# A bidirectional recurrence in rounds: tensor products regrouped and the round's order rewritten, on one core

## The chip, the cores and the metric

The kernel runs on one core of a Trainium2 chip. The metric is the device time of one execution in microseconds (us). The median of three runs of the kernel before is 2963.27 us (2956.47 to 2969.37).

The core has engines that each run their own instruction queue in order: PE (TensorE, matrix products; its weight loads are listed apart as PEld), DVE (VectorE), ACT (ScalarE), POOL (GpSimd) and SP (SyncE, which issues transfers). They wait for each other only through semaphores. A product reads its operands from SBUF and writes to PSUM, which has eight banks of 128 partitions x 512 fp32 numbers; DVE or ACT then bring it back to SBUF.

## The reference, cut to what matters

Two blocks run one after the other on 512 token rows of 1024 numbers. The change touches only the `rwkv_mixer` of the second block: a delta rule scan over 256 context tokens and then 512 tokens, with 8 heads of 64 numbers, once in each direction. A step is

```python
s_kk = jnp.einsum('bhvk,bhk->bhv', s, kk_t)
s = (s * w_t[:, :, None, :]
     - s_kk[..., None] * (kk_t * a_t)[:, :, None, :]
     + v_t[..., None] * k_t[:, :, None, :])
y = jnp.einsum('bhvk,bhk->bhv', s, inp[5]) if emit else None
```

For the context tokens only the state is needed, for the 512 others y as well. Both directions are summed; group norm, a bonus term and a gate follow (`rwkv_out`).

## The kernel before

The scan is done in chunks of L = 64 tokens: NCH = 12 rounds, numbered c = 0 to 11, each with one chunk of either direction. Rounds 0 to 3 are context; from c = 4 a chunk emits y (`emits(c)`). There are 2 directions x 8 heads = 16 problems of 64 x 64, kept as 8 tiles of 64 columns with two problems in each, one on partitions 0 to 63 and one on 64 to 127 (two of the array's 64-row groups). All products are fp32.

What a round computes, by the program's names (lines are those of the kernel before):

- **Pairs** of chunk n = c + 1, from scaled keys kt and bt (POOL, DVE), scaled directions kap and queries rho (POOL): AT = bt x kap, CT = kt x kap, and if it emits R1 = kt x rho, R2 = bt x rho; kT, bT and vt are the keys and values turned, by products with a 64 x 64 identity (L2138 to L2173). DVE masks CT, R1 and R2 into SBUF (`masked`, L2427) and chooses XT out of AT (L2415); ACT copies AT, kT, bT and vt (L2023).
- **Levels** 1 to 5 of the inverse X of a triangular matrix for chunk c, each a chain: product Y of AT with X (`level_Y`), masked product by DVE (`level_y`, L2440), product W (`level_W`), an addition by DVE (`level_x`, L2448), and a 32 x 32 turn by DVE (L2452). Each comes in two halves d = 0, 1 of four tiles.
- **State** of chunk s = c - 1: G = kap x state + CT x vt, U = X x G, Z = kT x vt + bT x U, the new state (DVE: `state_add`, `state_decay`), and if it emits y = rho x state + R1 x vt + R2 x U. ACT copies G and U into SBUF (L2009), since the next product needs them as an operand.
- **Decays** of chunk c + 2: `lora_pe` (L2120), `logits`, `cumulate`, `key_mix` on DVE, tanh and exp on ACT, products on POOL.

All products come from one helper `tiles` (L2087, the matmul on L2094), called with ALONG or ACROSS. ALONG, the problem on partitions 0 to 63 writes PSUM partitions 0 to 63, ACROSS it writes 64 to 127: in a pair of matmuls ALONG uses the two diagonal 64 x 64 quadrants of the array, ACROSS the two others. `beside` (L2105) interleaves an ALONG product (the levels) with an ACROSS product, a tile of each in turn, so that all four quadrants have work; `alone` runs one product. The order of a round is written out by hand for each engine (`rwkv_pe` from L2274, `rwkv_dve` from L2514, `rwkv_act` from L2053). A round of PE begins with `keep_clock(pe, 2, 4)`, four 128 x 128 products whose result nobody reads (L236).

After the loop PE makes half of a projection, turns the normalised y by 64 products ACROSS with the small identity (L2661), and goes on with the projection.

Of the kernel before, what the change touches and what calls it, by code (L numbers as in the profile page):

```python
# [14 lines left out]
P = 128  # L15
# [83 lines left out]
def hybrid_block_kernel(nc, stream, par, x_t, mod_w, c_rows, vbias, gate_w, masks, ctx_t, rpb, router_w, lora, experts, spill, gates_dram, xs_dram, ys_dram, out):  # L99
    ctx = ExitStack()  # L100
    with ctx:
# [1744 lines left out]
        kap, rho = [take(W8, "b") for _ in range(3)], [take(W8, "b") for _ in range(3)]  # L1846
# [3 lines left out]
        CT, R1, R2 = ([take(W8, "a") for _ in range(2)] for _ in range(3))  # L1850
# [28 lines left out]
        M_BANK = dict(vt=6, AT=4, CT=6, kT=4, bT=5, R1=6, R2=4)  # L1879
        LAST_C = NCH - 1  # L1880
        G_BANK = lambda c: 4 if c == LAST_C else 7
        U_BANK = lambda c: 5 if c == LAST_C else 7
        Y_BANK = lambda c: 6 if c == LAST_C else 7
# [18 lines left out]
        pe_m = Marks("rwkv_pe_pairs", lambda c: ("AT", "CT", "kT", "bT") + (("R1", "R2") if emits(c) else ()) + ("vt",))  # L1902
        pe_l = Marks("rwkv_pe_levels", lambda c: [f"{n}{l}{d}" for l in LV for n in "YW" for d in range(2)])
        pe_s = Marks("rwkv_pe_state", lambda c: ("Gs", "ys", "G", "yv", "U", "y") if c == LAST_C else ("Gs", "G", "U", "Z") + (("ys", "y") if emits(c) else ()))
# [4 lines left out]
        dve_p = Marks("rwkv_dve_decay", lambda c: "t0 t1 cs0 ka0 cs1 ka1 kd0 bt0 kd1 bt1 pl0 pl1".split())  # L1909
        dve_m = Marks("rwkv_dve_pairs", lambda c: ("XT", "X", "CT", "R1", "R2") if emits(c) else ("XT", "X", "CT"))  # L1910
# [26 lines left out]
        def rwkv_pool(pool):  # L1937
# [11 lines left out]
            for c in range(NCH):  # L1949
# [21 lines left out]
                for d in range(2):  # L1971
                    pool.wait_ge(dve_p.sem, dve_p.at(c, f"kd{d}"))
                    if c and d == 0:
                        pool.wait_ge(pe_m.sem, pe_m.at(c - 1, "R1" if emits(c - 1) else "kT"))
                    pool.tensor_tensor(half(kt, d), half(tk, d), half(pinv, d), ALU.mult).then_inc(pool_p.sem, 1)
# [13 lines left out]
        def rwkv_act(act):  # L1989
# [17 lines left out]
            def state_copy(c, name, bank, dst):  # L2007
                act.wait_ge(pe_s.sem, pe_s.at(c, name))
                act.activation(dst, psum[:, bank(c), :], ACT.Copy).then_inc(act_s.sem, 1)  # L2009

            def y_copy(c):
                if first_sum(c):
                    act.wait_ge(pe_s.sem, pe_s.at(c, "y"))
                    for d in range(2):
                        act.activation(y_chunk(c, d), half(psum[:, 7, :], d), ACT.Copy).then_inc(act_s.sem, 1)
# [7 lines left out]
            def pair_copy(c, name, dst):  # L2023
                act.wait_ge(pe_m.sem, pe_m.at(c, name))
                act.activation(dst[c % 2], psum[:, M_BANK[name], :], ACT.Copy).then_inc(act_m.sem, 1)
# [19 lines left out]
            pair_copy(0, "AT", AT)  # L2045
            pair_copy(0, "kT", kT)
            pair_copy(0, "bT", bT)
# [5 lines left out]
            for c in range(NCH):  # L2053
                more, next_too = c + 1 < NCH, c + 2 < NCH
                if c:
                    state_copy(c - 1, "G", G_BANK, Gs)
                pair_copy(c, "vt", vt)
                if c:
                    state_copy(c - 1, "U", U_BANK, Us)
                if more:  # L2060
                    unit(c + 1)
                    pair_copy(c + 1, "AT", AT)
                if next_too:
                    sigmoid_in(c + 2, 0)
                    sigmoid_in(c + 2, 1)
                    decays(c + 2, 0)
                if more:
                    pair_copy(c + 1, "kT", kT)
                if c:
                    y_copy(c - 1)  # L2070
                if more:
                    pair_copy(c + 1, "bT", bT)
                if next_too:
                    decays(c + 2, 1)
                if c + 3 < NCH:
                    lora_in_act(act, c + 3)
            rwkv_before_out_act(act)
            state_copy(LAST_C, "G", G_BANK, Gs)
            state_copy(LAST_C, "U", U_BANK, Us)
            rwkv_out_act(act)  # L2080

        def rwkv_pe(pe):
# [4 lines left out]
            ACROSS, ALONG = 1, 0  # L2087

            def tiles(n, bank, *terms, start=None, at=None, wide=L):
                first = n * L if at is None else at  # L2090
                for i, (way, lhs, rhs) in enumerate(terms):
                    for h in range(2):
                        r, o = ROWS[h], ROWS[h ^ way]
                        ins = pe.matmul(psum[o, bank, first:first + wide], lhs(n)[r], rhs(n)[r],  # L2094
# [1478 lines left out]
```

## Time and profile before

| | |
|---|---|
| median of three runs | 2963.27 us |
| profiled execution, its own time | 2955.09 us |
| its span | 2953.5 us |
| loop of the 12 rounds, from the 20 clock products of round 0 (2050.4) to the projection (2354.0) | 303.6 us |
| PE busy in the span | 2781.9 us, 94% |
| mean granted TensorE clock | 0.983 of full speed |

Busy time is the union of an engine's instructions. The view by stretches (rows 2) gives for each stretch its length, then for PE, PEld, DVE, ACT and POOL the busy time with the number of records, then the granted clock, the busy share of the transfer engines and the GB/s. A row of an engine in order of time gives start, duration, engine, line, operation, operands, shape and count, and in brackets how long the engine sat idle before it and what released it ("issue": nothing that the profile shows). A matmul's record begins where it starts to stream and its end is modelled, so the cost of one in a row of many is read from where the next begins. An fp32 matmul has two records of PE and two of PEld in this trace; a whole-array turn in transpose mode has one and one.

### The profile page before, as it was taken

What the parts mean: (1) busy time and instruction counts of PE and PEld (TensorE: products, weight loads), DVE (VectorE), ACT (ScalarE), POOL (GpSimd) and SP (SyncE); (2) the same over time, 40 slices, a digit from 0 to 9 for tenths busy, and PEclk for the clock granted to TensorE, in tenths of its full rate; (3) what the DMA queues carried; (4) which work ended last, traced back from release to release, by engine and by line L of the source; (5) the groups of instructions that cost most, each with busy time, mean ns of one, the idle gap of its engine ahead of it and who ended that gap; (6) DMA issues with size and microseconds to landing.
All of it is one profiled execution on the core that took longest, in us unless ns stands there. A gap on an engine that the chain in (4) does not pass through costs nothing. (4 is left out here: it accounts for less than half of the span.)

```text
span 2953.5 us, 55577 instructions
## 1 busy us (share of the span) xinstructions
PE 2781.9 (94%) x22194; PEld 2295.2 (78%) x22194; DVE 1782.0 (60%) x2735; ACT 1416.3 (48%) x1906; POOL 885.3 (30%) x535
## 2 busy tenths in 40 slices
PE   9999999989999999999999999899878899999997
PEld 7888877777777878888887788677777777888886
DVE  3114655877999953311165620667766655999995
ACT  4444544565663242344455322445433322888883
POOL 3444463130003434344443224342322233000001
PEclk9999999999999999999999999999999999999998
DMA  3334572111222223323274113232000043999995
GB/s 139 97 95 159 176 273 77 61 48 61 83 89 86 94 64 129 96 97 99 93 255 160 51 58 99 72 108 73 4 4 4 23 141 144 398 411 412 412 412 230
DMA packets 110389, 412.46 MB, mean 140 GB/s; under 512 B 12064, under 2 KB 12080, under 8 KB 109312
## 3 DMA queue, kind: packets, MB, share of 16 engines
q1 hardware_dynamic: 88560, 322.24, 30.4%
q0 software_dynamic: 11136, 48.26, 4.4%
q10 hardware_dynamic: 10512, 39.33, 3.7%
q8 instruction: 141, 2.31, 0.3%
q14 instruction: 40, 0.33, 0.0%
HBM read 370.45 MB, written 39.32 MB: 139 GB/s over the span
## 5 line engine op out<-in xcount | busy, mean ns | idle before, releaser
L219 POOL TENSOR_TENSOR ring_r<-ring,whi 128x1024 fp32r<-128x1024 f32 x241 | 592.6, 2469 | 891.0 <-ACT whi L214 881.8
L231 PE MATMUL psum<-xn_r,whi 128*128 128x512 f32 x1176 | 459.2, 390 | 0.0
L214 ACT ACTIVATE whi<-ring 128x1024 fp32r<-128x1024 f32 x247 | 255.8, 1055 | 398.1 <-DMA ring<-stream 394.6
L229 PE MATMUL psum<-xh,ring_r 128*128 128x512 f32 x936 | 385.2, 412 | 16.5 <-DVE ring_r L219 12.3
L2980 DVE TENSOR_TENSOR er_r<-er,eh 128x1024 fp32r<-128x1024 f32 x268 | 310.4, 1220 | 1.6 <-ACT eh L2969 0.7
L2969 ACT ACTIVATE eh<-er 128x1024 fp32r<-128x1024 f32 x268 | 269.2, 1071 | 44.3 <-DMA er<-experts 43.1
L229 PE MATMUL psum<-ffn_xh,ring_r 128*128 128x512 f32 x672 | 261.4, 389 | 0.0
L230 PE MATMUL psum<-ffn_xh,whi 128*128 128x512 f32 x672 | 261.4, 389 | 0.0
L231 PEld LDWEIGHTS psum<-xn_r,whi 128*128 128x128 f32 x1176 | 221.3, 188 | 47.1
L2094 PE MATMUL psum<-mem 64*64 64x64 f32 (+1 forms) x7744 | 203.3, 223 | 55.3 <-issue 27.5
L2094 PEld LDWEIGHTS psum<-mem 64*64 64x64 f32 x7744 | 188.0, 137 | 69.4 <-issue 44.7
L229 PEld LDWEIGHTS psum<-xh,ring_r 128*128 128x128 f32 x936 | 178.0, 190 | 70.1 <-DVE ring_r L219 15.1
L595 DVE TENSOR_TENSOR gu<-gu,psum 128x512 f32<-128x512 f32 x44 | 30.3, 688 | 333.4 <-ACT gu L570 333.4
L230 PE MATMUL psum<-xh,whi 128*128 128x512 f32 x504 | 197.4, 392 | 0.0
L230 PE MATMUL psum<-xh,whi_h 128*128 128x512 f32 x432 | 171.0, 396 | 0.0
L231 PE MATMUL psum<-xn_r,whi_h 128*128 128x512 f32 x432 | 170.9, 396 | 0.0
L498 DVE TENSOR_TENSOR mem<-mem 128x1024 f32<-128x1024 f32 x64 | 121.6, 1933 | 55.8 <-ACT mem L479 55.5
L3040 PE MATMUL psum<-er_r,xbh 128*128 128x512 f32 x368 | 147.0, 400 | 3.6 <-DVE er_r L2980 2.0
L229 PEld LDWEIGHTS psum<-ffn_xh,ring_r 128*128 128x128 f32 x672 | 126.1, 188 | 26.2
L230 PEld LDWEIGHTS psum<-ffn_xh,whi 128*128 128x128 f32 x672 | 126.1, 188 | 26.1
L3042 PE MATMUL psum<-eh,xbl 128*128 128x512 f32 x368 | 144.7, 393 | 0.0
L3041 PE MATMUL psum<-eh,xbh 128*128 128x512 f32 x368 | 144.3, 392 | 0.0
(532 smaller groups left out, 6041.7 us busy)
## 6 DMA issues: line engine op xcount, KB each, us to landing
ring<-stream SPq DMA_DIRECT2D x311, 512.0 KB, 3.5
er<-experts SPq DMA_DIRECT2D x276, 512.0 KB, 8.7
mem<-mod_w ACTq DMA_DIRECT2D x48, 512.0 KB, 4.3
xs_dram<-zero_row POOLq DMA_DIRECT2D x1, 12288.0 KB, 44.0
xs<-xs_dram SPq DMA_DIRECT2D x23, 512.0 KB, 8.6
ys_dram<-y_t ACTq DMA_DIRECT2D x23, 512.0 KB, 6.6
spill<-resid POOLq DMA_DIRECT2D x2, 2048.0 KB, 27.4
resid<-spill POOLq DMA_DIRECT2D x2, 2048.0 KB, 9.5
```

The costliest lines, as they stand in the source:

```text
L214: act.activation(high_of(part, j), w, ACT.Copy).then_inc(w_hi, 1)
L219: pool.tensor_tensor(ring_r[:, s, :, :], ring[:, s, :, :], f(high_of(part, j)), ALU.subtract).then_inc(w_lo, 1)
L229: pe.matmul(bank, lo[:, b, :], x_hi_, start=start, stop=False, skip_group_check=True)
L230: pe.matmul(bank, hi[:, b, :], x_hi_, start=False, stop=False, skip_group_check=True)
L231: return pe.matmul(bank, hi[:, b, :], x_lo_, start=False, stop=stop, skip_group_check=True)
L498: dve.tensor_tensor(mod_t[at % 2], mod_wb[m % 4], mod_c[:, s, :], ALU.mult).then_inc(mod_mul, 1)
L2094: ins = pe.matmul(psum[o, bank, first:first + wide], lhs(n)[r], rhs(n)[r], start=i == 0 if start is None else start, stop=i == len(terms) ...
L2969: act.activation(eh[:, SLOT[kind] + j, :], er[:, SLOT[kind] + j, :], ACT.Copy).then_inc(e_hi, 1)
L2980: dve.tensor_tensor(er_r[:, at, :], er[:, at, :], f(eh[:, at, :]), ALU.subtract).then_inc(e_lo_dve, 1)
L3040: pe.matmul(bank, x_hi_, lo_[:, cols], start=start, stop=False, skip_group_check=True)
L3041: pe.matmul(bank, x_hi_, hi_[:, cols], start=False, stop=False, skip_group_check=True)
L3042: return pe.matmul(bank, x_lo_, hi_[:, cols], start=False, stop=stop, skip_group_check=True)
```

## The change

`tiles` becomes three helpers. `tiles` keeps the ALONG form. `to_tokens` runs pair i = 0 to 7 of problems, where even i writes ALONG and odd i ACROSS, the two problems of a pair into two neighbouring banks; in the operands that have tokens on partitions (CT, R1, R2, AT, vt, Gs, Us) heads of a pair of tiles therefore lie in another order ("slots"). `to_keys` is its counterpart on the way back. kT and bT are turned by four whole-array transposes each (128 x 128, in transpose mode) instead of 16 products with the small identity. Where a chunk emits, CT and R1 are one product of kt with kap and rho side by side (128 columns: `CR`), and AT and R2 one of bt (`AR`). `keep_clock` at the round's start, and `beside` inside the rounds (but for the last), are gone; Z and y are split into a part that needs U and one that doesn't; `lora_pe` runs one round earlier, at a round's end. DVE and ACT follow: masks and copies read two banks by slots, CR is masked by two operations of 128 x 512, R2 and the choice of XT by two of 128 x 256 each. In `rwkv_out_pe` 16 whole-array transposes take the place of the 64 products.

```diff
-            def tiles(n, bank, *terms, start=None, at=None, wide=L):
+            def tiles(n, bank, lhs, rhs, start=True, at=None, wide=L):
...
+            def to_tokens(i, banks, lhs, rhs, start=True, wide=L, every=L):
+                a, odd = i // 2, i % 2
+                for h in range(2):
+                    n = 2 * a + (h ^ odd)
+                    ins = pe.matmul(psum[ROWS[h ^ odd], banks + h, a * every:a * every + wide], lhs(n)[ROWS[h]], rhs(n)[ROWS[h]],
+                                    start=start, stop=True, skip_group_check=True)
+                return ins
...
+            def turned(bank, src):
+                return lambda a: pe.transpose(psum[:, bank, a * P:(a + 1) * P], src[:, a * P:(a + 1) * P], ident[:, :])
...
+            def pair_CR(c):
+                W(pool_p, c, "kt1")
                 if c:
                     W(act_m, c - 1, "vt")
+                if c >= 2:
+                    W(act_s, c - 2, "U")
+                keys = keys_of(c)
+                return lambda n: to_tokens(n, M_BANKS, of(kt), keys, wide=2 * L if emits(c) else L, every=2 * L)
...
             def state_y_old(c):
                 if c < LAST_C:
-                    W(dve_s, c, "z")
+                    W(act_s, c, "G")
...
             for c in range(NCH):
                 n, s = c + 1, c - 1
-                    keep_clock(pe, 2, 4)
-                    level_Ys(c, 1, state_G_old(s), pe_s)
-                    alone(state_G_new(s), ALL, pe_s)
+                level_Ys(c, 1)
+                if last:
+                    alone(state_G_old(s), ALL, pe_s)
+                level_Ws(c, 1)
+                if last:
+                    alone(state_G_new(s), ALL, pe_s)
+                alone(pair_vt(c), ALL, pe_m)
+                level_Ys(c, 2)
+                if y:
+                    alone(state_y_old(s), ALL, pe_s)
+                level_Ws(c, 2)
+                if last:
+                    alone(state_U(s), ALL, pe_s)
+                level_Ys(c, 3)
+                if more:
+                    alone(pair_CR(n), ALL, pe_m)
+                level_Ws(c, 3)
+                if last:
+                    alone(state_Z_values(s), ALL, pe_s)
+                if y:
+                    alone(state_y_values(s), ALL, pe_s)
+                level_Ys(c, 4)
+                if last:
+                    alone(state_Z(s), ALL, pe_s)
+                level_Ws(c, 4)
+                if y:
+                    alone(state_y(s), ALL, pe_s)
+                if more:
+                    alone(pair_AR(n), ALL, pe_m)
+                level_Ys(c, 5)
+                    level_Ws(c, 5)
+                    if c + 3 < NCH:
+                        lora_pe(c + 3)
+                    alone(pair_kT(n), PAIRS, pe_m)
+                    alone(pair_bT(n), PAIRS, pe_m)
...
             def pair_CR(c):                       # on DVE
+                wait(pe_m, c, "CR")
+                if emits(c - 2):
+                    wait(pe_s, c - 2, "yv")
...
+                    dve.tensor_tensor(to, pairs_of(d)[:, :, :, 0:m], over_slots(mask_CR[:, d, 0:m]), ALU.mult).then_inc(dve_m.sem, 1)
```

First place, PE at the start of a round that emits. Before (L236 are the clock products, 64x32 the levels, `shared,mem` the turn of the values, L2133 the decays' `lora_pe`):

```order
L236 MATMUL psum<-ones 128x128 x4
L2094 MATMUL psum<-mem 64x32 x2
L2094 MATMUL psum<-mem 64x64 x2
...
L2094 MATMUL psum<-mem 64x32 x2
L2094 MATMUL psum<-mem 64x64 x18
L2133 MATMUL psum<-mem,shared 128x64 x16
L2094 MATMUL psum<-mem 64x32 x2
L2094 MATMUL psum<-shared,mem 64x64 x2
...
L2094 MATMUL psum<-mem 64x32 x16
L2094 MATMUL psum<-mem 64x64 x16
```

After (L2111 is `tiles`, L2119 `to_tokens`, L2127 `to_keys`):

```order
L2111 MATMUL psum<-mem 64x32 x16
L2119 MATMUL psum<-mem 64x64 x16
L2111 MATMUL psum<-mem 64x32 x16
L2111 MATMUL psum<-mem 64x64 x16
L2119 MATMUL psum<-shared,mem 64x64 x16
L2111 MATMUL psum<-mem 64x32 x16
L2119 MATMUL psum<-mem 64x64 x16
L2111 MATMUL psum<-mem 64x32 x16
L2111 MATMUL psum<-mem 64x64 x16
L2111 MATMUL psum<-mem 64x32 x16
L2119 MATMUL psum<-mem 64x128 x16
L2111 MATMUL psum<-mem 64x32 x16
```

The clock products, the decays' 16 products and the interleaving are gone from here; each product now stands as a block between two halves of a level.

Second place, PE at the end of the same kind of round, after:

```order
L2119 MATMUL psum<-mem 64x128 x16
L2111 MATMUL psum<-mem 64x32 x32
L2177 MATMUL psum<-mem,shared 128x64 x16
L2132 MATMUL psum<-ident,mem 128x128 x8
L2111 MATMUL psum<-mem 64x32 x16
```

The product of 128 columns is AR, then come both parts of level 5, the decays, now for chunk c + 3, and the eight transposes of kT and bT, where before R1 and R2 were interleaved with level 5.

Third place, DVE from level 3 to level 5. Before (L2417 chooses XT, L2392 and L2390 are `cumulate`, L2429 the masks, L2458 and L2464 the state):

```order
L2440 TENSOR_TENSOR mem<-psum,shared 128x128 x2
...
L2417 COPY_PREDICATED mem<-shared,psum 128x2x256
L2392 SCALAR_TENSOR_TENSOR resid<-mem,zero_row 128x256
L2448 TENSOR_TENSOR mem<-mem,psum 128x16x8 x2
...
L2458 TENSOR_TENSOR mem<-mem,psum 128x512
L2429 TENSOR_TENSOR mem<-psum,shared 128x512
...
L2464 TENSOR_TENSOR mem<-mem 128x512
L2390 SCALAR_TENSOR_TENSOR resid<-mem,zero_row 128x256
L2440 TENSOR_TENSOR mem<-psum,shared 128x4x32 x2
...
```

After (L2445 masks CR, L2451 chooses XT, L2463 masks R2, L2493 and L2499 are the state):

```order
L2412 SCALAR_TENSOR_TENSOR resid<-mem,zero_row 128x256
L2483 TENSOR_TENSOR mem<-mem,psum 128x16x8 x2
...
L2445 TENSOR_TENSOR mem<-psum,shared 128x512 x2
L2475 TENSOR_TENSOR mem<-psum,shared 128x128 x2
...
L2493 TENSOR_TENSOR mem<-mem,psum 128x512
L2499 TENSOR_TENSOR mem<-mem 128x512
L2475 TENSOR_TENSOR mem<-psum,shared 128x4x32 x2
...
L2451 COPY_PREDICATED mem<-shared,psum 128x256 x2
L2463 TENSOR_TENSOR mem<-psum,shared 128x256 x2
L2483 TENSOR_TENSOR mem<-mem,psum 128x4x32 x2
L2456 STREAM_TRANSPOSE mem<-mem 128x2x256
```

The state's two operations now stand before level 5's first, the choice of XT has moved from level 3 to level 5, and the masks of CT and R1 are one pair of operations in level 3.

## Rows read from the trace of the kernel before

**Rows 1.** the page: busy time; PE and granted clock in 40 slices (tenths)

```profile
PE 2781.9 (94%) x22194; PEld 2295.2 (78%) x22194; DVE 1782.0 (60%) x2735; ACT 1416.3 (48%) x1906; POOL 885.3 (30%) x535
PEclk9999999999999999999999999999999999999998
```

**Rows 2.** busy time: rounds 0; 1-2; 3; 4; 5-9; 10; 11; tail

```profile
2050.40:2072.20 21.80, 18.21 (x525) 17.43 (x521) 18.60 (x47) 12.96 (x29) 10.88 (x13) 0.92 0.02 5
2072.20:2114.30 42.10, 35.67 (x1362) 33.27 (x1360) 31.82 (x92) 18.38 (x39) 12.54 (x17) 1.00 0.02 4
2114.30:2136.20 21.90, 18.02 (x749) 16.77 (x745) 16.09 (x47) 9.32 (x21) 8.08 (x11) 1.00 0.02 4
2136.20:2160.90 24.70, 18.51 (x747) 17.07 (x745) 17.14 (x49) 9.25 (x20) 7.86 (x11) 1.00 0.01 4
2160.90:2291.90 131.00, 104.39 (x4204) 97.40 (x4201) 85.90 (x241) 48.70 (x102) 38.70 (x51) 0.99 0.02 5
2291.90:2319.30 27.40, 18.95 (x811) 17.58 (x808) 14.95 (x46) 4.10 (x7) 4.50 (x7) 1.00 0.05 13
2319.30:2344.80 25.50, 22.91 (x694) 20.48 (x694) 15.44 (x41) 9.69 (x13) 12.81 (x8) 0.87 0.02 4
2344.80:2354.00 9.20, 9.09 (x147) 5.91 (x136) 4.05 (x7) 5.06 (x9) 2.32 (x2) 1.00 0.01 2
```

**Rows 3.** waits in the loop: us in total, times, longest

```profile
DVE mem L2448 <- PE psum L2094: 67.7, 56, 4.3
PE psum L2094 <- issue: 30.2, 33, 1.8
DVE mem L2440 <- PE psum L2094: 24.5, 43, 1.7
```

**Rows 4.** PE in order of time: start, us, ..., count, idle before it

```profile
2092.16 1.12 PE L2094 MATMUL psum<-mem 64*64 64x32 f32 x32 [0.80 <-DVE mem L2440]
2093.21 1.16 PE L236 MATMUL psum<-ones 128*128 128x128 f32 x8
...
2095.64 1.15 PE L2094 MATMUL psum<-mem 64*64 64x64 f32 x32 [0.18 <-PE psum L2094]
2096.71 2.00 PE L2133 MATMUL psum<-mem,shared 64*128 64x64 f32 x32
...
2203.87 0.39 PE L2094 MATMUL psum<-mem 64*64 64x64 f32 x8 [1.45 <-issue]
...
2219.29 0.25 PE L2094 MATMUL psum<-mem 64*64 64x32 f32 x2
...
2220.33 4.69 PE L2094 MATMUL psum<-mem 64*64 64x32 f32 x202
...
2365.41 3.95 PE L2661 MATMUL psum<-shared,mem 64*64 64x64 f32 x128
...
2630.30 0.60 PE L3034 MATMUL psum<-ident,hid_t 128*128 128x128 f32 x4
2630.74 1.04 PE L3027 MATMUL psum<-ident,xs 128*128 128x128 f32 x8
```

**Rows 5.** DVE in order of time, round 6

```profile
2195.48 0.29 DVE L2448 TENSOR_TENSOR mem<-mem,psum 128x128 f32<-128x128 f32 x1 [2.59 <-PE psum L2094]
...
2196.94 0.48 DVE L2440 TENSOR_TENSOR mem<-psum,shared 128x128 f32<-128x128 f32 x2
...
2205.96 0.68 DVE L2429 TENSOR_TENSOR mem<-psum,shared 128x512 f32<-128x512 f32 x1
```

**Rows 6.** ACT in order of time, a copy of U

```profile
2197.95 0.60 ACT L2009 ACTIVATE mem<-psum 128x512 f32<-128x512 f32 x1 [1.35 <-PE psum L2094]
```

**Rows 7.** transfer queues over the loop: queue, packets, MB

```profile
q8 instruction: 73, 1.20, 1.7%
```

**Rows 8.** transfers of 2204 to 2226 in 40 slices, GB/s

```profile
GB/s 0 0 30 0 0 0 0 0 0 30 0 0 0 0 15 30 0 0 0 0 0 0 30 0 0 0 0 0 30 0 0 0 0 0 0 30 0 0 0 0
q8 instruction: 6, 0.10, 1.8%
```

More of the change, by code:

```diff
@@ L1845, in hybrid_block_kernel @@
         half = lambda v, d: bd(v[:, 4 * L * d:4 * L * (d + 1)])
-        kap, rho = [take(W8, "b") for _ in range(3)], [take(W8, "b") for _ in range(3)]
+        kap_rho = [take(2 * W8, "b") for _ in range(3)]
+        kap, rho = [v[:, 0:W8] for v in kap_rho], [v[:, W8:2 * W8] for v in kap_rho]
         bt, kt = take(W8, "b"), take(W8, "b")
@@ L1849, in hybrid_block_kernel @@
         XX = [take(2 * W8, "a") for _ in range(2)]
-        CT, R1, R2 = ([take(W8, "a") for _ in range(2)] for _ in range(3))
+        CR = [take(2 * W8, "a").rearrange("p (n w t) -> p n w t", n=8, w=2) for _ in range(2)]
+        R2 = [take(W8, "a") for _ in range(2)]
         kT, bT, vt = ([take(W8, "b") for _ in range(2)] for _ in range(3))
@@ L2085, in rwkv_pe @@
             tile_ = lambda v, n: v[:, n * L:(n + 1) * L]
-            ACROSS, ALONG = 1, 0
-            def tiles(n, bank, *terms, start=None, at=None, wide=L):
+            def tiles(n, bank, lhs, rhs, start=True, at=None, wide=L):
                 first = n * L if at is None else at
[L2091 to L2094, printed above, removed]
-                                        start=i == 0 if start is None else start, stop=i == len(terms) - 1, skip_group_check=True)
-                return ins
+                for r in ROWS:
+                    ins = pe.matmul(psum[r, bank, first:first + wide], lhs(n)[r], rhs(n)[r],
+                                    start=start, stop=True, skip_group_check=True)
+                return ins
@@ L2126, in lora_pe @@
                 W(act_w, c, "lw")
-                for m in range(2):
+                for m in parts:
                     for q in range(4):
@@ L2215, in state_U, with state_Z_values @@
                 W(act_s, c, "G")
[L2216 to L2218 removed]
+                if c < LAST_C:
+                    W(act_m, c + 1, "vt")
+                return lambda n: tiles(n, U_BANK, XT_of(c), of(Gs))
+            def state_Z_values(c):
+                W(dve_p, min(c + 3, NCH - 1), "t1")
+                W(act_m, c, "vt")
+                return lambda n: to_keys(n, Z_BANKS, of(kT[c % 2]), of(vt[c % 2]), start=n < 2)
@@ L2230, in state_y_old, with state_y_values @@
-                return lambda n: tiles(n, Y_BANK(c), (ACROSS, of(rho[c % 3]), of(st[c % 2])), start=n == 0)
-            def state_y_new(c):
-                W(dve_m, c, "R2")
+                return lambda n: to_tokens(n, Y_BANKS(c), of(rho[c % 3]), of(st[c % 2]), start=n < 2)
+            def state_y_values(c):
+                W(dve_m, c, "CR1")
                 W(pe_s, c, "ys")
-                return lambda n: tiles(n, 7, (ALONG, of(R1[c % 2]), of(vt[c % 2])), (ALONG, of(R2[c % 2]), of(Us)), start=False)
@@ L2247, in level_Ys @@
-            def level_Ys(c, l, other=None, done=None):
+                return lambda n: slot_product(n, Y_BANKS(c), of(R2[c % 2]), of(Us))
+            def level_Ys(c, l):
                 for d in range(2):
-                    y = level_Y(c, l, d)
-                    if other is None:
-                        alone(y, (LOW, HIGH)[d], pe_l)
-                    else:
-                        beside(y, (LOW, HIGH)[d], pe_l, other, (LOW, HIGH)[d], done if d else None)
+                    alone(level_Y(c, l, d), (LOW, HIGH)[d], pe_l)
@@ L2255, in rwkv_pe, with level_Ws @@
+            def level_Ws(c, l):
+                for d in range(2):
+                    alone(level_W(c, l, d), LOW, pe_l)
             pe.wait_ge(na_a.sem, na_a.end())
```

389 lines of the change are left out of this document (187 added, 202 removed).

## The prediction

> **What bounds the kernel now.** I read the page first. PE is busy 94% of the span, and the granted clock is at or near full speed in all slices [rows 1], so the whole program is close to PE's speed, and an engine's share says nothing more. Then the view by stretches, which cuts the loop at the clock products that open each round [rows 2]. Here PE is less busy than elsewhere: a context round (1 and 2) takes 21.05 us with PE busy 17.8, a full round (5 to 9, those that make pairs, state and y) 26.2 us with PE busy 20.9. DVE is second with 15.9 and 17.2. So neither is full, and the round is a chain that goes to and fro between them. Nothing of the later program can start before the loop ends, so a round that is shorter by 1 us is 1 us of the kernel.
>
> Third, the waits inside the loop [rows 3]. DVE waits for PE 67.7 us before the additions of the levels and 24.5 before their masks. PE itself sits idle 30.2 us in 33 places where no engine released it. One such place is the 1.45 us before 2203.87 [rows 4]. I take these for the supply of PE's instructions, for three reasons. The queue that carries instructions brings 73 packets of 16 KB into the loop [rows 7]. The records of PE and PEld in the eight stretches add up to 9,239 and 9,210 [rows 2], 253 per packet. And in a dense stretch the packets come at a beat: six in 22 us, 3.7 us apart [rows 8]. A full round has 841 + 841 records, 6.6 packets, hence 24.2 us at that beat, of 26.2. A context round has 681 + 680, 5.3 packets, 19.7 of 21.05. By this reading PE is short of instructions for much of the loop: where four quadrants run interleaved it uses 128 records in 1.04 us (2219.29 to 2220.33, [rows 4]), a packet in 2.1 us, far faster than they come.
>
> The Trainium skill says the contrary in "Runtime: NRT & Kernel Launch", section "Instruction fetch mechanics": blocks of 256 instructions are fetched ahead and the fetch is hidden, because dispatch is slower than the fill. The packet size agrees with the trace (253 records per packet), that it is hidden doesn't (30.2 us of idle time with no releaser). By that rule fewer instructions would bring nothing of themselves, and only the array's time below would count.
>
> **The change part by part, for a full round.** Unit prices on PE, from where the next row begins [rows 4]:
>
> - Half levels, 32 columns ALONG, alone: 32 records (16 matmuls) from 2092.16 to 2093.21, 1.05 us. The other places where I looked gave down to 0.95; I take 1.0.
> - 64 columns ALONG, alone: 2095.64 to 2096.71, 1.07.
> - A level beside an ACROSS product: 64 records in 1.04. So the second product is free there, and a level alone costs as much as a level with company.
> - `to_tokens` and `to_keys`, 16 matmuls that alternate the diagonals: not in the trace. The order of quadrants is that of `beside`, 32 matmuls in 1.04, hence 0.53 for 16. Upper bound 1.07, if they don't overlap. I take 0.53, since the quadrants follow each other in the same way.
> - The same with 128 columns (CR, AR): not in the trace. Lower bound 0.53 (as 64 columns), upper 2.1 (twice the price of 64 alone). Columns count: four 128-column clock products take from 2093.21 to about 2094.3, 0.27 each, and there would be four groups of four quadrants; I take 1.07.
> - Decays: 1.9 to 2.0 as before, only moved. Whole-array transpose: four from 2630.30 to 2630.74, 0.11 each, so kT and bT cost 0.87 for the eight.
>
> Sum of PE, before: clock products 1.1; level 1 first half with G old 1.05; G new 1.07; decays 1.95; vt, AT, CT, kT, bT, R1, R2 and old y beside levels, 8 x 1.05 with the split levels counted; U 1.0; Z of two ACROSS terms beside level 3 2.1; level 2 alone 1.0; new y 2.1. That is 19.8, and rows 2 have 20.9, so this way of counting may be 1 us low, for the new round too; that lies in the range. After: ten levels 10.0; G old, vt, old y, both parts of Z 5 x 0.53 = 2.65; G new, U, y from values, y from U 4.3; CR and AR 2.15; decays 1.95; transposes 0.87. Together 21.9. **So the array's work does not fall; it rises by about 1 us.** Instructions do: 360 products of which 8 have half the records, 1,424 against 1,684. That is 5.6 packets, 20.6 us at 3.7 us each, under the 21.9 of the array. The supply stops being the longer of the two.
>
> What remains to wait. DVE has 17.2 + 0.2 (masks in halves) a round, below PE's 21.9, and its idle time costs nothing. CR needs Us copied by ACT, 0.2 + 0.60 [rows 6] behind the tanh pair of the next decays; level 3's first half of 1.0 on PE covers most of it. DVE's mask of CR waits for y from values; behind it stand level 4's masks, for which PE waits some 0.3. I put 0.4 on such dependencies and 0.9 (the mean of the 33 idle places, 30.2 / 33) on one supply gap: a full round takes 21.9 + 1.3 = 23.2. DVE's idle time before additions falls from single waits like 2.59 us [rows 5], since a level's two products are now split by one block, not by decays and two state products.
>
> The sum, against rows 2:
>
> - rounds 5 to 9: 131.0 to 116, -15.0
> - rounds 1 and 2: PE 10.0 + 6 x 0.53 + 2.1 + 2.8 = 18.1, and DVE's state operations (0.6 each, like [rows 5] 0.68) now stand before level 5, where PE has little else: +1.0. Two of 19.1: -3.9
> - round 3: wide CR and AR +1.07, a little supply, 20.1: -1.8. Round 4 the same, 20.1: -4.6
> - round 10, without decays: 21.9 - 1.95 + 1.5 = 21.4: -6.0
> - round 11: levels 10.0, state 6.9, bonus 1.2, waits 2.5 = 20.6: -4.9; the clock stood at 0.87 there, what that does next is open; I take -4.5
> - round 0: kT and bT no longer alone: -1.0
> - after the loop: 64 products 3.95 us to 16 transposes 16 x 0.11 = 1.75 [rows 4]: -2.0; the projection behind it keeps PE without a gap, so it counts.
>
> Together -38.8. A second way: over the loop there are 684 fp32 products fewer (clock products counted) and 96 transposes more, 684 x 4 - 96 x 2 = 2,544 records or 10 packets, and at 3.7 us (the beat) to 4.2 (303.6 / 73) a packet that is 37 to 42 us, if supply were all, and the 2 after the loop beside it. Between the two I take **-40**. The profiled execution took 2955.1 (span 2953.5 and 1.6 around it), 8.2 under the median; the sum is a difference, so I take it off the median: 2963.3 - 40 = **2923 us**.
>
> **The rivals.**
>
> - *DVE becomes the bound.* If the supply gaps are the real price and levels alone go at 0.85, PE falls to 20 a round and the round is DVE's 17.4 + 2.5 of halves that it waits for. That gives 20 for rounds 5 to 9 and 18 for the context rounds, in all -65: 2898. For it: DVE waits 92 us for PE in two lines [rows 3]. Against it: PE's own sum.
> - *Waits take it back.* Each round gets 3 us of new waits: ACT's copies of G and U now gate old y and CR, and stand in ACT's queue between tanh operations; and every W half now waits for its mask with nothing interleaved. 12 x 3 = 36: 2959, no change. For it: round 4 already takes 24.7 us with PE busy 18.5, more than either engine's work or the supply explains. Against: ACT is busy 9.7 of 26 us.
> - *The diagonals don't overlap* (the slower one). Place: `to_tokens` and `to_keys` in every round. Price: 5 x 0.54 + 2 x 1.07 = 4.8 us in a full round, 23.2 to 28.0 against 26.2; 6 x 0.54 = 3.2 in a context round, 22.3 against 21.05. In all 5 x 1.8 + 2 x 1.3 + 2.5 (round 3) + 0.6 (round 10) less 3 after and before: about +12, 2975. It turns into a loss from 3.0 us a round on, that is when more than 60% of the overlap is missing. Against it: `beside` shows the overlap with the same quadrants.
> - *The clock falls.* The loop had dips already, 0.92 in round 0 and 0.87 in round 11 [rows 2], and the clock products are gone. At the low level (1.2 GHz) each us of PE's work costs one more; the 40 us are lost when 40 of the loop's some 250 us of PE work run low. With all of it low: 2923 + 250 = 3173; I carry it with half, 3050. Against it: the rounds that gain have PE busier, 94% against 80%. The Trainium skill, "TensorE: Matmul & The Clock Gate", section "Part 4: PE-mode transpose", says that transposes don't count as PE activity for the clock; by it the 0.87 us of transposes behind each round would be idle for the gate. No row here shows that.
>
> **How the numbers follow.** Forecast 0.56, DVE bound 0.15, waits take it back 0.18, no overlap 0.07, clock 0.04. The forecast's own range is 2905 to 2942 (waits of 0 to 3 us a full round, levels at 0.95 to 1.05). The range for 8 in 10 reaches from the upper part of the DVE case to the lower part of the waits case: 2887 to 2956. A change of 0.5%, 15 us, is what a measurement of this kernel can tell from none. Faster by more: 0.56 + 0.15 + half of the waits case, 0.80. Slower: 0.07 + 0.03, 0.10. The same: 0.10.
>
> **What would show it.** Right: rounds 5 to 9 at 22 to 24 us with PE busy 21 or more; the idle time of PE without releaser falls from 30 to 15 us or less; 63 packets of instructions in the loop instead of 73; 32 records of `to_tokens` in 0.53 us, of CR in about 1.07. Wrong: those blocks at 1.07 and 2.1; PE's idle time released by ACT before old y or CR; a granted clock under 0.95 in rounds 1 to 10; or the instruction packets at a beat under 3 us, which would take the supply out of the explanation.

## The result, and the profile after

The kernel after takes 2945.48 us (median of 8 runs, 2931.01 to 2955.78), the kernel before beside it 2963.77 us (8 runs, 2952.48 to 2969.37): ratio 0.9946, 95% interval 0.9927 to 0.9965. That is 16 to 18 us faster. The forecast was 40 us faster. The profiled execution took 2940.7 us against 2955.1 before.

Three lines of the page of after: the span, the engines, and the clock over the span.

```profile
span 2939.1 us, 52834 instructions
...
PE 2802.9 (95%) x20810; PEld 2321.8 (79%) x20810; DVE 1776.2 (60%) x2759; ACT 1410.1 (48%) x1906; POOL 880.9 (30%) x535
...
PEclk9999999999999999999999999999889999999998
```

[Rows 1] had PE at 94%. Two slices of the loop now stand at 8 tenths in PEclk. The view by stretches of after says where. Its columns are those of [rows 2]. The stretches are round 0 from the decays of round 1 on; rounds 1 and 2; 3; 4; 5 to 9; round 7 alone; 10; 11 up to the output's gate product.

```profile
2049.60:2083.20 33.60, 29.41 (x604) 28.08 (x600) 21.46 (x58) 13.83 (x31) 11.24 (x14) 0.82 0.01 3
2083.20:2130.00 46.80, 43.73 (x1234) 41.90 (x1232) 30.95 (x96) 17.94 (x39) 13.04 (x18) 0.82 0.02 4
2130.00:2153.10 23.10, 21.78 (x618) 20.92 (x616) 16.57 (x50) 8.65 (x20) 7.20 (x10) 0.85 0.01 3
2153.10:2174.80 21.70, 20.33 (x618) 19.60 (x616) 16.54 (x50) 9.01 (x20) 7.20 (x10) 0.91 0.02 4
2174.80:2285.80 111.00, 106.72 (x3530) 103.16 (x3528) 86.31 (x249) 46.18 (x102) 36.43 (x50) 0.97 0.02 5
2221.50:2243.70 22.20, 21.06 (x714) 20.37 (x712) 17.15 (x51) 9.52 (x22) 7.24 (x10) 1.00 0.02 4
2285.80:2308.40 22.60, 19.47 (x682) 18.62 (x680) 15.53 (x49) 3.88 (x8) 2.36 (x4) 1.00 0.06 15
2308.40:2337.30 28.90, 25.66 (x810) 22.18 (x809) 15.78 (x41) 13.44 (x20) 14.69 (x8) 1.00 0.02 4
```

Against [rows 2]: rounds 5 to 9 fall from 131.0 to 111.0 us (one of the decays, 2 us, has left them for round 0). Rounds 1 and 2 rise from 42.1 to 46.8, round 3 from 21.9 to 23.1, round 4 falls from 24.7 to 21.7. The last column but two is the granted clock. Before it was 1.00 in rounds 1 to 4, now it is 0.82, 0.85 and 0.91. Taking 1 minus this clock, times the stretch, times two, gives the time at half clock (the 1.2 GHz level). By stretches of 1 us, which round less than these rows, it is 47.8 us in the loop of after and 13.7 in that of before.

The waits in the loop of after, for [rows 3] (lines 2475 and 2483 are the mask and the addition of the levels, 2111 the products):

```profile
DVE mem L2475 <- PE psum L2111: 40.0, 54, 5.0
...
DVE mem L2483 <- PE psum L2111: 26.8, 67, 3.9
...
PE psum L2111 <- issue: 5.8, 14, 0.9
```

PE's idle time without releaser went from 30.2 us in 33 places to 6.1 in 15 (5.8 before products of `tiles`, 0.3 before one of `to_keys`), and the loop now takes 64 instruction packets where it took 73. DVE's idle time before additions fell from 67.7 to 26.8, before masks it rose from 24.5 to 40.0, as levels now follow their masks with less between them.

PE's timeline of after shows the prices that the trace of before could not show: CR with 128 columns, from 2230.18 to where the level behind it starts, 0.89 us; a `to_tokens` block, from 2244.63 to 2245.23, 0.60; the 16 transposes of the output, to the next row, 1.67 where [rows 4] had 3.95.

```profile
2230.18 1.10 PE L2119 MATMUL psum<-mem 64*64 64x128 f32 x32
2231.07 1.04 PE L2111 MATMUL psum<-mem 64*64 64x32 f32 x30
...
2244.63 0.27 PE L2119 MATMUL psum<-mem 64*64 64x64 f32 x2
...
2244.73 0.66 PE L2119 MATMUL psum<-mem 64*64 64x64 f32 x30
2245.23 0.96 PE L2111 MATMUL psum<-mem 64*64 64x32 f32 x28
...
2351.70 1.91 PE L2696 MATMUL psum<-ident,mem 128*128 128x128 f32 x16
2353.37 0.48 PE L229 MATMUL psum<-ybh,ring_r 128*128 128x512 f32 x1
```

So the array's prices were near (0.89 where 1.07 was taken, 0.60 where 0.53 was), and yet more than half of the gain is missing. The clue is what PE does just ahead of a dip of the clock. From the timeline of PE, one wait in round 0, the end of round 1, and the end of round 2:

```profile
2076.85 1.06 PE L2111 MATMUL psum<-mem 64*64 64x32 f32 x30 [0.86 <-DVE mem L2475]
...
2096.56 1.10 PE L2111 MATMUL psum<-mem 64*64 64x32 f32 x31
2098.82 1.55 PE L2111 MATMUL psum<-mem 64*64 64x32 f32 x32 [1.16 <-DVE mem L2475]
2100.30 3.68 PE L2177 MATMUL psum<-mem,shared 64*128 64x64 f32 x32
...
2124.56 1.12 PE L2111 MATMUL psum<-mem 64*64 64x32 f32 x32 [1.17 <-DVE mem L2475]
2125.61 2.80 PE L2177 MATMUL psum<-mem,shared 64*128 64x64 f32 x32
```

DVE at the end of round 1 (L2493 and L2499 are the state, L2475 the last masks):

```profile
2097.19 0.65 DVE L2493 TENSOR_TENSOR mem<-mem,psum 128x512 f32<-128x512 f32 x1
2097.87 0.69 DVE L2499 TENSOR_TENSOR mem<-mem 128x512 f32<-128x512 f32 x1
2098.48 0.48 DVE L2475 TENSOR_TENSOR mem<-psum,shared 128x128 f32<-128x128 f32 x2
```

And by stretches, the idle one, the dip behind it (end of round 1 and start of round 2), and the dips ahead of round 0 and in it, from round 2 to 3, and from round 4 to 5:

```profile
2097.66:2098.80 1.14, 0.00 (x0) 0.00 (x0) 1.11 (x4) 0.68 (x3) 0.39 (x1) 1.00 0.00 0
2099.30:2113.00 13.70, 13.70 (x230) 13.19 (x229) 5.39 (x19) 1.82 (x4) 1.52 (x2) 0.50 0.01 2
...
2048.10:2061.80 13.70, 10.91 (x143) 10.48 (x144) 6.06 (x12) 4.94 (x10) 3.47 (x5) 0.50 0.00 1
2126.60:2136.80 10.20, 10.20 (x180) 9.75 (x181) 3.98 (x15) 1.48 (x3) 1.52 (x2) 0.50 0.01 3
2171.00:2181.20 10.20, 10.20 (x168) 9.75 (x170) 4.48 (x16) 1.20 (x2) 1.77 (x3) 0.50 0.01 2
```

PE has nothing to do for 1.16 us before the last level product (its mask stands in DVE's queue behind the state operations of the round), and then it runs at half clock: the decays take 3.68 us instead of 2.00 [rows 4]. In three of the four dips PE is busy all the time, so its work costs double; in the first it is busy for 10.9 of 13.7 us.

Such an idle stretch is not enough by itself. In round 0 one of 0.86 us, before 2076.85, has no dip behind it. In the kernel before PE idles for 0.6 us or more 45 times in the loop, 22 times for 1 us or more, among them the 1.45 us of [rows 4], and its loop has only 3.4, 3.4 and 6.8 us at half clock. Why one idle stretch is followed by a dip and another isn't, no run here shows. Whether filling them helps can be tried.

The eight runs of after say the same of the price: their mean granted clock goes from 0.970 (2955.78 us) to 0.980 (2931.01 us), with a correlation of -0.99 between clock and time, 2.5 us per 0.001. The median is 0.974; for before it is 0.981 over the 17 runs beside the first experiments.

### The profile page after: what moved, and what is told of

Same layout as the page of the kernel before. It is cut to its first block and busy times, and to the rows that moved or that the text cites. A ratio compares the mean times of both kernels' runs of the same rounds, so it can differ in the third digit from the quotient of the medians.

```text
span 2939.1 us, 52834 instructions
## 1 busy us (share of the span) xinstructions
PE 2802.9 (95%) x20810; PEld 2321.8 (79%) x20810; DVE 1776.2 (60%) x2759; ACT 1410.1 (48%) x1906; POOL 880.9 (30%) x535
## 5 line engine op out<-in xcount | busy, mean ns | idle before, releaser
L2111 PE MATMUL psum<-mem 64*64 64x32 f32 (+1 forms) x5120 | 180.6, 224 | 18.0 <-DVE mem L2475 9.7
L2111 PEld LDWEIGHTS psum<-mem 64*64 64x64 f32 x5120 | 171.0, 141 | 27.3 <-issue 12.9
```

Of the source, the lines that this page charges most:

```text
L2111: ins = pe.matmul(psum[r, bank, first:first + wide], lhs(n)[r], rhs(n)[r], start=start, stop=True, skip_group_check=True)
```

## The experiments

Ratios are to the kernel before on the same chip (medians 2957.9, 2958.1 and 2957.8 us in the three groups).

### Clock products back at each round's start: clock_each_round

```diff
+                if last:
+                    ...
+                    fill_clock(pe, 4)     # 128-column products into bank 6
                 level_Ys(c, 1)
```

> The kernel after, with the four clock products that the kernel before had at the start of rounds 1 to 11 put back (128 columns each, into a bank that nobody reads then). They are 44 products, 0.27 us each by rows 4 of the kernel before, so 12 us of added array work. Theory A (the gain is lost to the clock, and it was these products that held it up): the time at half clock in the loop falls from 47.8 us in the profile of after to 15 or less, which gives back 17 us, less the 12 added: 2940 us. Rival B (the dips come from stalls elsewhere in the round, which four products at its start don't touch): the dips stay near 48 us and the products cost what they take, 2955 to 2957 us. Rival C (dips are an accident of a run and cost nothing of note): like B in time.

Measured: 2943.3 us, ratio 0.9950 (0.9931 to 0.9969), no different from after. Its profile (a run at 0.975) still has 44.4 us at half clock in rounds 0 to 4. Theory A in this form fell. But rival B, which wanted 2955 to 2957 us, did not come true either: the 12 us that the products cost do not show, and the median clock of its runs is 0.978 against 0.974, which at 2.5 us per 0.001 is about 10 us. At this place, where PE isn't idle, they give back about what they cost.

### Clock products where PE stands idle: fill_the_stalls

```diff
-            keep_clock(pe, 0, 48)
+            keep_clock(pe, 0, 58)
...
             alone(pair_AR(0), ALL, pe_m)
+            fill_clock(pe, 8)
...
                 if more:
+                    if c < 5:
+                        fill_clock(pe, 4)
                     level_Ws(c, 5)
```

> The kernel after, with clock products only where PE stands idle just before its clock falls: ten more before the CR product of round 0 (idle 2.67 us there), eight before level 1 of round 0 (idle 2.25 us), and four before the last level product of rounds 0 to 4 (idle about 1.16 us in rounds 2 and 3). Nearly all of them lie in idle time. Theory A (these idle stretches let the clock fall): time at half clock in the loop falls from 47.8 to 15 us or less, and the kernel takes 2928 to 2932 us. Rival B (the clock follows something else, such as the share of transposes or of small products): the dips stay near 48 us and the time stays at 2945 to 2949 us.

Measured: 2925.0 us, ratio 0.9892 (0.9873 to 0.9911), 16 us better than after, as theory A had it. (The idle stretches of 1.16 us stand at the ends of rounds 1 and 2, not in 2 and 3.) The median granted clock is 0.982. In its profile, rounds 0; 1 and 2; 3; 4; 5 to 9; 7 alone; 10; 11:

```profile
2049.00:2080.20 31.20, 28.16 (x627) 26.56 (x624) 21.68 (x58) 13.86 (x31) 11.23 (x14) 1.00 0.02 3
2080.20:2121.90 41.70, 38.35 (x1250) 36.94 (x1248) 31.38 (x96) 17.50 (x39) 13.02 (x18) 1.00 0.02 4
2121.90:2142.10 20.20, 19.86 (x626) 19.09 (x624) 16.55 (x50) 8.70 (x20) 7.19 (x10) 1.00 0.02 4
2142.10:2162.30 20.20, 19.89 (x626) 19.11 (x624) 16.55 (x50) 8.69 (x20) 7.20 (x10) 1.00 0.02 4
2162.30:2269.30 107.00, 103.08 (x3531) 99.84 (x3528) 86.74 (x249) 46.44 (x102) 36.72 (x50) 1.00 0.02 5
2205.20:2227.20 22.00, 21.07 (x714) 20.31 (x712) 17.67 (x51) 9.56 (x22) 7.40 (x10) 1.00 0.02 5
2269.30:2291.40 22.10, 20.07 (x682) 19.17 (x680) 15.99 (x50) 4.15 (x8) 2.20 (x4) 0.96 0.05 16
2291.40:2322.40 31.00, 29.07 (x810) 25.70 (x809) 15.18 (x39) 13.38 (x20) 14.69 (x8) 0.86 0.02 4
```

The clock is 1.00 from round 0 to round 9; with more work than after in every one of them, rounds 0 to 4 take 113.3 us instead of 125.2. A dip of 10.2 us is left, later, in rounds 10 and 11. The end of round 2, now filled:

```profile
2116.91 1.16 PE L241 MATMUL psum<-ones 128*128 128x128 f32 x8
2118.00 1.12 PE L2116 MATMUL psum<-mem 64*64 64x32 f32 x32
2119.05 0.66 PE L2182 MATMUL psum<-mem,shared 64*128 64x64 f32 x8
```

The wait for the mask is gone. An idle stretch of 0.76 us without releaser still stands just ahead of it (before 2116.74), and has no dip behind it.

### Its two halves: fill_rounds_only, fill_start_only

The first keeps only the line before `level_Ws(c, 5)`, the second only the two edits ahead of the loop.

> The kernel after with only one part of fill_the_stalls: four clock products before the last level product of rounds 0 to 4. In fill_the_stalls all of it together took the half-clock time in the loop from 47.8 to 10.2 us and gave a ratio of 0.9892 to before, against 0.9946 for after. Theory A1 (each idle stretch answers for the dip that follows it): the dip at 2048 stays (13.7 us), those at 2099, 2126 and 2171 go; 34 us less at half clock is 17 us less time at most, 10 by what fill_the_stalls shows per us: ratio 0.990 to 0.992. Rival A2 (the prologue's dip alone starts the others): nothing is gained, ratio 0.9945.

> The kernel after with only the other part of fill_the_stalls: ten more clock products before the CR product of round 0 and eight before its level 1. Theory A1: the dip at 2048 goes and those of rounds 1 to 4 stay, 34 us at half clock; 13.7 us less of it is 5 to 7 us less time, ratio 0.992 to 0.993. Rival A2 (the first dip sets off the others): all go, ratio 0.9892.

Measured: 0.9897 (0.9883 to 0.9912) for the products in the rounds, 0.9951 (0.9937 to 0.9965) for those at the start. The first bring all of it, within the intervals, the second nothing. A1 was right for the time of the rounds and wrong for the start: there the dip at 2048 us went, but dips came at 2093, 2120, 2145, 2192 and 2328 us, 47.8 us at half clock in all. A dip that is prevented in one place can come back at another; only filling the wait that recurs each round gained time.

The dips of fill_rounds_only are not as A1 had them. Its profile is of its slowest run (2941.8 us at a mean clock of 0.977; the other three have 0.981 to 0.983) and still has 34.1 us at half clock: 10.2 from 2051 us on, and 23.9 from 2072 to 2096, across the end of round 0, where one of the fillings stands. So, by the clocks of the runs, the filling makes such dips rarer, and does not rule them out.

### Transposes replaced by products: turn_by_products

```diff
-                return turned(T_BANK["kT"], kt)
+                return lambda n: to_tokens(n, 4, of(kt), lambda n: two_ident)
```

(and for bT at columns 256 on, with ACT's copies to match)

> The kernel after, with kT and bT made by 64-wide products with the identity that alternate the diagonals (2 x 16 products) instead of 2 x 4 whole-array transposes; ACT copies kT once bT is done too. By the prices in the profile of after it adds 2 x 0.59 less 0.87, 0.3 us a round, and 2 x 56 instructions, near half a packet a round. Theory A (idle stretches set the clock): the dips stay at 40 to 55 us, and the time is 3 to 8 us longer: 2948 to 2953 us. Rival T (transposes do not count as activity, so that the 0.87 us of them at each round's end lets the clock fall): the dips after the round's end go, below 20 us in all, and the time falls to 2932 to 2937 us. Rival S (supply of instructions is still tight): 11 x 0.45 packets x 3.7 us = 18 us longer, 2963 us.

Measured: 2943.5 us, ratio 0.9951 (0.9935 to 0.9967), 44.4 us at half clock in its profile. Rival T is out: without transposes the dips stay. So is S at this size (0.45 packets a round): from decays to decays its full rounds at full clock take 22.1, 22.4 and 22.5 us, those of after 22.1 to 22.2.

### The kernel before without its clock products: before_no_clock

```diff
-                    keep_clock(pe, 2, 4)
                     level_Ys(c, 1, state_G_old(s), pe_s)
```

> The kernel before without its four clock products at the start of rounds 1 to 11. They took 12 us of the array (44 x 0.27) and 176 records. Theory A (they hold the clock): 12 us are saved, and the time at half clock in the loop rises from 13.6 us to 40 or more, which gives about 13 us back: 2960 to 2967 us, no change. Rival B (they hold nothing up): the dips stay at 10 to 20 us and the kernel takes 2950 to 2953 us; then the 12 us of the forecast's sum that came from taking them away were real.

Measured: 0.9995 (0.9984 to 1.0006). The time at half clock in its profile rises from 13.7 to 34.1 us, and the median granted clock is 0.9785 against 0.981. By the time it is theory A: 12 us of work off, and 0 to 3 us gained. The clock accounts for about 10 us by the two profiles, for some 5 by the medians (2 us per 0.001); the rest is open. In before, then, the products do their work; the forecast's sum had booked their removal as pure gain.

### The supply of instructions

The dips could be all of the story, and supply none. Three runs test the reading of before as bound by PE's instructions, and a fourth the overlap of the diagonals. First a cut in before:

```diff
-  (ACROSS, of(kt), of(rho[c % 3])))
+  (ACROSS, of(kt), of(rho[c % 3]))) if n == 7 or c == LAST_C else None
```

(the same for R2; new y from `XT_of(c)`)

> The kernel before with 14 of the 16 products of R1 and 14 of R2 left out in rounds 3 to 9 (of the pairs of rounds 4 to 10; y then is computed from other tiles of the same shapes). They stood beside the two halves of level 5, where the trace has them at no cost of the array (64 records in 1.04 us beside a level, 32 in 1.05 alone). It is 112 records less of 1,684 in a round, 784 in all, 3.1 packets. Theory S (before is bound by the supply of PE's instructions, at 3.7 us a packet): 11 us less, ratio 0.996, and rounds 5 to 9 at 24.6 us instead of 26.2; PE's idle time without releaser falls. Rival W (the rounds of before are bound by its chain of level products, copies and state): 0 to 2 us less, ratio 0.9993 to 1.

Measured: 1.0005 (0.9994 to 1.0015), so by its number rival W. The waits say more: in rounds 5 to 9 PE's idle time without releaser fell from 15.2 us in 18 places to 8.2 in 8. But the five rounds together got longer, 135.1 us against 131.0, at a granted clock of 0.90 (0.99 before), and at the low clock part of this idle time may vanish by itself. Counting the time at half clock half, as an estimate, they are 121.6 against some 129.5, 1.6 us a round less, what S wanted. The median clock over its runs is 0.978 against 0.982; at about 2 us per 0.001, that is some 8 us back. This run alone decides nothing; the next two start from fill_the_stalls, whose clock in rounds 5 to 9 is 1.00 in its profile, as it is in theirs.

```diff
+            def with_extra(level, ones, c):
+                for i, n in enumerate(ones):
+                    extra(c)(i)      # two 64x64 products, other diagonal, bank 6/7 from column 256
+                    ins = level(n)
+                ins.then_inc(pe_l.sem, 1)
```

> fill_the_stalls with 48 extra products (64x64, of keys with the identity, into columns that nobody reads) in each of rounds 5 to 10, one beside each product of the second half-levels of 2 and 3 and the first of 3, on the other diagonal. In the trace of before, 64 records so interleaved took 1.04 us and 32 alone 1.05, so the array should not notice them. They are 192 records a round (1,424 become 1,616, near the 1,684 of before), 4.5 packets in all. Theory S (PE's instructions come at 3.6 us a packet and bound a full round once it has 6.4 of them): rounds 5 to 9 go from 21.5 to about 23 us, 9 us in all, ratio 0.992 to 0.993, and PE's idle time without releaser grows by several us. Rival W (the supply bounds nothing; the rounds of before were long through their dependencies): rounds 5 to 9 stay within 0.5 us of 21.5, ratio 0.989 to 0.990.

(The extra products open sums in the banks in which the old part of y stands, so y comes out different.)

Measured: 0.9964 (0.9950 to 0.9978). And the change's widest part undone:

```diff
-                return lambda n: to_tokens(n, M_BANKS, of(kt), keys, wide=2 * L ...)
+                def both(n):
+                    to_tokens(n, M_BANKS, of(kt), of(kap[c % 3]), every=2 * L)
+                    return to_tokens(n, M_BANKS, of(kt), of(rho[c % 3]), every=2 * L, shift=L)
+                return both
```

> fill_the_stalls with one part of the change undone: every CR and AR block of keys and queries made by two products of 64 columns each instead of one of 128. It is 128 records more in a round with queries (3 to 10), 1,552 in a full one, 8 x 0.5 packets. On the array a block of 32 matmul records took 0.59 us at 64 columns and 0.9 to 1.1 at 128, so two of 64 are 0.1 to 0.3 us more than one of 128. Theory S: rounds 5 to 9 at 22.0 to 22.5, 5 to 8 us in all, ratio 0.991 to 0.992. Rival W: 8 x 0.3, 2.4 us, ratio 0.990; then the 128-column product itself brought next to nothing.

Measured: 2945.9 us, 0.9962 (0.9948 to 0.9976). Rounds 5 to 9 of more_records by stretch:

```profile
2159.90:2281.30 121.40, 106.49 (x4010) 101.29 (x4008) 87.82 (x249) 46.70 (x102) 36.92 (x50) 1.00 0.02 5
```

of two_64_columns, by stretch, and PE's waits there:

```profile
2163.70:2282.10 118.40, 105.92 (x3850) 101.75 (x3848) 86.12 (x249) 46.32 (x102) 36.32 (x50) 1.00 0.02 4
```

```profile
PE psum L2116 <- issue: 4.0, 8, 0.9
PE psum L2132 <- issue: 3.6, 5, 1.1
PE psum L2124 <- issue: 3.0, 5, 1.0
```

107.0 us became 121.4 with 192 records more a round, and 118.4 with 128 more. PE's busy time grew by only 3.4 and 2.8 us; the rest, 11.0 and 8.6 us, is idle, and 9.7 and 8.5 of that is idle time without releaser. That is theory S, and more than it asked: a round grew by 2.9 us for 0.76 packets and by 2.3 for 0.51, where 1.5 and 0.5 to 1 were expected. By the idle time alone it is 2.2 / 0.76 = 2.9 and 1.7 / 0.51 = 3.4 us a packet, somewhat under the beat of 3.7 [rows 8]. So the expectation erred in taking rounds of 1,424 records for free of the supply; they stand near its edge. Not every record costs the same: turn_by_products has 112 more than after in a round and its full rounds grew by 0.2 us. Why the place matters wasn't tried. By the profiles the 128-column product brings some 18 us (8 rounds of 2.3, an estimate), three quarters of it through the instructions that it saves. The ratios give 21 us; the median clock of two_64_columns is 0.979 against 0.982, some 6 of them.

> fill_the_stalls with the tiles of every to_tokens and to_keys block in the order 0, 2, 4, 6, 1, 3, 5, 7, so that a diagonal of the array is used four times in a row instead of the two in turn. The instructions are the same. If the low price of these blocks (0.59 us for 16 products of 64 columns in the profile of after, 1.07 alone on one diagonal in that of before) comes from alternating the diagonals, each block costs about 0.5 us more and CR and AR 1 us more: 4.5 us a full round, some 3 in the others, 40 to 46 us in all, ratio 1.003 to 1.006, slower than before. If instead it comes from anything else, the ratio stays at 0.989.

The fourth run, diagonals_apart, measured 0.9896 (0.9877 to 0.9915), as fill_the_stalls. Rounds 5 to 9 take 108.8 us against 107.0. The expectation was wrong by 40 us: the order within a block matters little. In the trace the level behind such a block starts 0.57 us after the block does (2196.36 to 2196.93), while the second diagonal is still at work, so four tiles in a row on one diagonal are no obstacle; the products behind them on the other diagonal go on.

### Decays into the first wait: decays_first

```diff
-            alone(pair_CR(0), ALL, pe_m)
             lora_pe(1)
+            alone(pair_CR(0), ALL, pe_m)
```

> fill_the_stalls with lora(1), 2.0 us of PE's work, ahead of the CR product of round 0 instead of behind it. CR waits there for POOL's second key tile, 2.67 us in the trace of after. If lora(1)'s inputs are there by then, it runs inside that wait and 1.5 to 2 us are saved: ratio 0.9885, hardly to be told from 0.9892. If PE is at the time waited for by DVE instead (CR's mask comes later), it is 0 to 2 us longer, ratio 0.9895.

Measured: 2920.9 us, ratio 0.9883 (0.9866 to 0.9901). It is the fastest here, 35 us under before; its 2 to 3 us over fill_the_stalls lie within the intervals. Its profile has no dip in the loop at all, though PE idles there for 1.0, 1.1 and 1.9 us at a time.

## Why the prediction was wrong

The sign was right, and so was the mechanism of the gain, fewer instructions at about the same work for the array. The size was not: -40 was forecast, -16 to -18 measured. The step that failed is the last rival, "the clock falls", which had 0.04, and with it the sum, which holds no term for a lower clock and books the clock products' removal as gain. The rival's price, each us of work at the low level costs one more, held. Its argument against itself, that the rounds that gain have PE busier, 94% against 80%, did not: in round 1 of after PE is busy for 12.3 of 12.7 us at full clock (2085.00 to 2097.66), then idle for 1.1, and the clock falls. In the profile of after the dips come ahead of round 0 and at the ends of rounds 1, 2 and 4, behind idle stretches of 0.77 to 2.8 us. Those in the rounds are places where the new order has nothing to put between DVE's late mask and the last level product. 34 us more at half clock should cost 17 us, half of them; 16 is what fill_the_stalls gives back. What makes the chip answer these idle stretches, and not the longer ones of before, stays open.

Point by point, with the clock held (fill_the_stalls, the terms from the profiles, the forecast in brackets):

- Rounds 5 to 9: -24.0 (-15.0). After itself -20.0, at a clock of 0.97. Round 7 of after at full clock takes 22.2 us, with PE busy 21.06; forecast 23.2 and 21.9. The waits are 1.1, not 1.3, and CR and AR cost 0.9 instead of 1.07.
- Rounds 1 and 2: -0.4 (-3.9). PE's own work is 18.1 a round as counted, once the 1.1 us of filling are taken off; idle time is 1.7 instead of 1.0.
- Round 3: -1.7 (-1.8); round 4: -4.5 (-4.6); round 10: -5.3 (-6.0).
- Round 11 with the tail: about -0.6 (-4.5). Most of the dip of 10.2 us lies here; in after, without it, this was -2.8.
- Start of the loop, from the clock products ahead of it (2031.10 in before, 2034.66 in fill_the_stalls) up to round 1: +4.4 (-1.0), in after +7.2. Two us of it are decays that moved in from round 1 on, booked nowhere in the forecast, though they left rounds 5 to 9. For the rest, CR(0), which needs POOL's last key tile, now stands ahead of AR(0): in after PE waits 2.8 us for it. That this is all of the rest isn't shown.
- Behind the loop: -2.6 (-2.0). In after it is -0.8, although the transposes themselves save 2.3 us there too; where that went wasn't tried.

The terms for the loop add up to -32.1, with the part behind it to -34.7. The two profiled executions differ by 31.1, since the loop starts 3.6 us later in that of fill_the_stalls, where 58 us ahead of it run at half clock against 51. The ratio says -32. So of the 24 us missing, 16 are the clock. The other 8 are by the profiles the start, the context rounds and the tail, less what the full rounds gave beyond the forecast, and some 4 that these single executions don't resolve (the rounding of the forecast among them).

The other rivals: DVE did not become the bound (17.2 of 22.2 us in round 7). "Waits take it back" was the nearest by its number, 2959 against 2945, but its reason was not the one: PE is idle less than before in rounds 1 to 10 (3.1 us against 6.4 in rounds 1 and 2). The diagonals overlap. On the fetch of instructions the forecast's reading held. Rounds 5 to 9 got 11.4 and 14.4 us longer with only 2.8 and 3.4 us more of PE's work. The Trainium skill, "Runtime: NRT & Kernel Launch", section "Instruction fetch mechanics", has the fetch hidden behind slower dispatch; with products as small as these the runs here contradict that. On the clock, the Trainium skill, "TensorE: Matmul & The Clock Gate", section "Part 4: PE-mode transpose", says that a transpose doesn't count as PE being busy in the way a product does. Had that set the dips, turn_by_products would have ended them; it still had 44.4 us.

Of the signs named ahead, idle time without releaser under 15 us (6.1), full rounds of 22 to 24 us with PE busy 21 (22.2 and 21.06) and fewer packets (64, where 63 were named) came true, and so did one of the signs of being wrong: a granted clock under 0.95 in rounds 1 to 4.

## What to carry to other kernels

When a reordering takes interleaved work away, look at the granted clock by stretches and at the single places where PE stands idle ahead of a dip, and not only at the busy share of a round: here four 128-column products in one such place in each of five rounds were worth about 15 us, nearly as much as the whole change had brought by itself. Which idle place matters could not be told from its length; try the filling. Where TensorE runs chains of small fp32 products, count the instructions per round beside the columns: 128 records more in CR and AR cost 2.3 us in a round of 21.4. Compare kernels together with the mean granted clock of each run, since it explains most of the scatter between runs.

## What the runs showed that had not been expected

- The places where PE idles without releaser stand at a fixed position of the instruction stream. In rounds 5 to 9 of before, the idle stretches ahead of 2171.61, 2175.54, 2203.87, 2225.99, 2229.36, 2242.80, 2254.22, 2262.66, 2266.53, 2278.62 and 2282.36 us are all a multiple of 256 records of PE and its queue apart, to within 3.
- Removing work can leave the time the same: before_no_clock and before_fewer_products both did less and took as long, at a lower mean clock.
- A kernel's dips differ from run to run: the eight runs of after have mean clocks of 0.970 to 0.980, and each account of single dips above rests on one profiled execution.
- Four tiles in a row on one diagonal of the array cost hardly more than two diagonals in turn (1.8 us over rounds 5 to 9), as long as the products behind them use the other one.
